# Last attention: dilated groups' scores on 128x32 tiles, queries stored by remainder modulo four, weights added on VectorE

## What is computed

```python
DILATED_GROUPS = ((128, 1), (512, 4), (2048, 16))      # (window, dilation)

def dilated_window_attention(q, k, v, window, dilation):
    """Causal dilated window: query t attends t, t-r, t-2r, ..., t-window.
    Returns normalised output and log-denominator."""
...
def dilated_layer(h, k, v, norm_g, w_in, qnorm_g, w_out, cos, sin):
    proj = rms_norm(h, norm_g) @ w_in
    q, z = jnp.split(proj, [B_QW], axis=-1)
    q = apply_rope(rms_norm(q, qnorm_g), cos, sin)      # 3 groups x 4 heads x 128
    outs, lses = [], []
    for g, (window, dilation) in enumerate(DILATED_GROUPS):
        o_g, l_g = dilated_window_attention(q[:, :, g], k, v, window, dilation)
        outs.append(o_g)
        lses.append(l_g)
    wts = jax.nn.softmax(jnp.stack(lses, axis=0), axis=0)
    o = jnp.einsum('gbsh,gbshd->bshd', wts, jnp.stack(outs, axis=0))
    y = o.reshape(Bsz, S, B_VW) * jax.nn.silu(z.astype(jnp.float32))
    return y.astype(h.dtype) @ w_out
```

## Time and profile before

| | |
|---|---|
| median of 3 runs | 1366.26 us (1366.13 to 1366.35) |
| the profiled execution | 1366.81 us, span in the trace 1365.0 us |
| PE busy | 1354.0 us, 99% of the span |
| DVE, ACT, POOL busy | 854.6, 609.3, 192.3 us |
| granted TensorE clock | 1.00 in each stage shown below |
| queries and attention of the last layer | about 1168 us to 1298 us of the span |

### The profile page before, as it was taken

How to read it: one execution, slowest core, us unless ns; L and a number is a source line. 1 busy time by engine, 2 the same in 40 slices (tenths; PEclk the granted TensorE clock), 3 DMA queues, 4 the chain that set the end, 5 groups by cost and what they waited for, 6 DMA issues and landing times.

```text
span 1365.0 us, 17389 instructions
## 1 busy us (share of the span) xinstructions
PE 1354.0 (99%) x6812; PEld 1108.2 (81%) x6812; DVE 854.6 (63%) x1243; ACT 609.3 (45%) x938; POOL 192.3 (14%) x166
## 2 busy tenths in 40 slices
PE   9999999999999999999999999999999999999998
PEld 7778787888888788888888888788888888787887
DVE  6565666855344797524777356747464666877775
ACT  5264433433245464323444355435554544444551
POOL 0300010222222200000000112011201210244330
PEclk9999999999999999999999999999999999999999
DMA  6322222323352443332333323522224233222132
GB/s 215 113 88 78 78 78 62 93 68 101 95 184 63 139 123 103 114 94 79 105 95 94 119 81 142 155 77 78 63 80 167 82 121 111 78 62 63 47 139 77
DMA packets 37818, 136.57 MB, mean 100 GB/s; under 512 B 4452, under 2 KB 5476, under 8 KB 37096
## 3 DMA queue, kind: packets, MB, share of 16 engines
q1 hardware_dynamic: 37440, 134.39, 31.7%
q10 hardware_dynamic: 296, 1.06, 0.2%
HBM read 129.14 MB, written 6.30 MB: 99 GB/s over the span
## 4 chain that ended last, share of the span: by engine, by line
PE 88%; DVE 8%; issue 1%; ACT 1%; DMA 1%; POOL 0%; DVEq 0%; SPq 0%; ACTq 0%; POOLq 0%
PE ps L205 86%; PE ps L209 3%; DVE WL L152 2%; DVE TT L164 2%; DVE HL L164 1%; DMA kept<-PW 1%; DVE X L152 1%; DVE sm L170 0%; DVE KT L164 0%; DMA raw<-in_wall 0%; ACT HH L202 0%; DVE gS L164 0%; ACT row L202 0%; DVE row L167 0%; ACT VT L202 0%
## 5 line engine op out<-in xcount | busy, mean ns | idle before, releaser
L205 PE MATMUL ps<-HH,WH 128*128 128x512 f32 (+1 forms) x1096 | 437.0, 401 | 1.1 <-DVE HL L164 0.6
L205 PE MATMUL ps<-HL,WH 128*128 128x512 f32 (+1 forms) x1096 | 423.4, 388 | 0.0
L205 PE MATMUL ps<-HH,WL 128*128 128x512 f32 (+1 forms) x1080 | 417.6, 388 | 0.0
L152 DVE TENSOR_TENSOR WL<-raw,WH 128x1024 fp32r<-128x1024 f32 (+1 forms) x221 | 282.1, 1282 | 77.5 <-ACT WH L189 73.4
L189 ACT CAST WH<-raw 128x1024 fp32r<-128x1024 f32 (+1 forms) x222 | 231.3, 1044 | 123.4 <-PE ps L205 101.8
L205 PEld LDWEIGHTS ps<-HH,WH 128*128 128x128 f32 x1096 | 206.4, 188 | 47.7 <-issue 5.1
L205 PEld LDWEIGHTS ps<-HL,WH 128*128 128x128 f32 x1096 | 206.1, 188 | 41.7 <-issue 1.9
L205 PEld LDWEIGHTS ps<-HH,WL 128*128 128x128 f32 x1080 | 202.8, 188 | 42.7
L205 PE MATMUL ps<-PH,WH 128*128 128x512 f32 x424 | 167.1, 394 | 0.0
L205 PE MATMUL ps<-PH,WL 128*128 128x512 f32 x424 | 165.2, 390 | 0.0
L205 PE MATMUL ps<-PL,WH 128*128 128x512 f32 x424 | 165.1, 389 | 0.0
(11 more groups left out here) (227 smaller groups left out, 1476.7 us busy)
## 6 DMA issues: line engine op xcount, KB each, us to landing
raw<-in_wall SPq DMA_DIRECT2D x221, 512.0 KB, 3.6
kept<-PW SPq DMA_DIRECT2D x2, 2048.0 KB, 9.1
PWR<-kept SPq DMA_DIRECT2D x2, 2048.0 KB, 8.3
X<-in_xT SPq DMA_DIRECT2D x8, 256.0 KB, 4.0
X<-in_xT SPq DMA_DIRECT2D x4, 512.0 KB, 5.3
out_T<-X SPq DMA_DIRECT2D x7, 256.0 KB, 2.0
pe<-in_pT SPq DMA_DIRECT2D x2, 512.0 KB, 4.6
MB<-mrow ACTq DMA_DIRECT2D x1, 1024.0 KB, 5.9
```

The costliest lines, as they stand in the source:

```text
L152: return self.put(None if self.e is None else self.e.tensor_tensor(out, x, y, op))
L205: return self.put(None if self.e is None else self.e.matmul(out, l, r, start=start, stop=stop, skip_group_check=True))
```

## The change

Three things are changed together.

1. Queries are stored by class. Within each block of 128 positions, `qt(h, g)` now holds first the 32 positions with remainder 0 modulo 4, then those with 1, 2 and 3 (`by_class`, `by_token`). This is done while writing: VectorE puts the cosine part into the scratch ring `TH` in natural order, and GpSimd's addition writes `QT` in class order. ScalarE's squares go out in class order too, and at the end of a head the factor and the output are brought back to natural order. ScalarE makes a copy `KC` of the keys, sorted by class over all 512 positions, one copy for each head.
2. `scores(i)`: group 0 stays one matmul of 128 queries by `W0` keys. For groups 1 and 2 each class `k` has a matmul of its own: 32 stationary columns (the class's queries), moving the `L/4` keys of that class, into partitions `32k` to `32k+31` of the bank. So eight matmuls take the place of two. All three groups of a step share one bank, and steps alternate between two banks. The score row shrinks from `W0 + 2L` to `W0 + L/2`, and with it the mask, the masking instructions and the exponential.
3. `merge(i)` moves from GpSimd to VectorE. Four additions, one for each class on its 32 partitions, write the sum of groups 1 and 2 to every fourth column of `PB` (zeroed once by GpSimd). A fifth adds the near columns of `PB` to group 0's weights, in place in `SS`. `turn(i)` transposes the near blocks from `SS` and the far ones from `PB`.

```diff
@@ att_sizes, att_groups @@
-            return L, W0, W0 + 2 * L
+            return L, W0, W0 + L // 2
...
-                w, k0 = (W0, L - W0) if g == 0 else (L, 0)
-                so = 0 if g == 0 else W0 + (g - 1) * L
-                mo = (0, 256, 768)[g] + (256 if g == 0 else 512) - w
-                yield g, w, k0, so, mo
+                w = L // 4 if g else W0
+                yield g, w, W0 + (g - 1) * w if g else 0, (256, 384, 512)[g] - w
+        def by_class(x):
+            return x.rearrange("p (n c j) -> p n j c", n=4, c=4)
+        def by_token(x):
+            return x.rearrange("p (n j c) -> p n j c", n=4, c=4)
@@ pe_program, attend: scores @@
-                    for g, w, k0, so, mo in att_groups(n):
-                        s = p.fill(SB[g], ("as", i, g))
-                        p.wait_ge(S.dve, "kt", h)
+                    s = p.fill(SB[i % 2], ("as", i))
+                    p.wait_ge(S.dve, "kt", h)
+                    p.wait_ge(S.act, "kc", h)
+                    for g, w, so, mo in att_groups(n):
                         p.wait_ge(S.pool, "rope", ("q", h, g))
-                        p.matmul(s[:, 0:w], qt(h, g)[:, n * P:(n + 1) * P], KT[:, h, k0:k0 + w],
-                                 True, True).then_inc(("as", i, g))
+                        if g == 0:
+                            p.matmul(s[:, 0:W0], qt(h, 0)[:, n * P:(n + 1) * P], KT[:, h, L - W0:L], True, True)
+                        else:
+                            for k in range(4):
+                                p.matmul(s[32 * k:32 * k + 32, so:so + w], qt(h, g)[:, n * P + 32 * k:n * P + 32 * k + 32],
+                                         KC[:, h, k * P:k * P + w], True, True)
+                    p.then_inc(("as", i))
@@ pe_program, attend: turn @@
-                    p.wait_ge(S.pool, "aw", i)
+                    p.wait_ge(S.dve, "aw", i)
                     for kb in range(n + 1):
-                        p.transpose(s[:, kb * P:(kb + 1) * P], PB[:, kb * P:(kb + 1) * P], ident)
+                        at0 = kb * P - (L - W0)
+                        p.transpose(s[:, kb * P:(kb + 1) * P], near[:, at0:at0 + P] if at0 >= 0 else PB[:, kb * P:(kb + 1) * P], ident)
@@ v_rope_q @@
-            v.scalar_tensor_tensor(u, ps(*name), gn, CS[:, 0, :], MUL, MUL)
+            v.take("TH", ("rope", name))
+            v.scalar_tensor_tensor(th_("rope", name), ps(*name), gn, CS[:, 0, :], MUL, MUL)
@@ dve_program, attend @@
-                            v.wait_ge(S.pool, "aw", i - 2)
-                        v.tensor_tensor_reduce(Sc[:, so:so + w], ps("as", i, g)[:, 0:w], DM[:, mo:mo + w],
+                            v.wait_ge(S.pe, "at", i - 2)
+                        v.tensor_tensor_reduce(Sc[:, so:so + w], ps("as", i)[:, so:so + w], DM[:, mo:mo + w],
...
+                def merge(i):
...
+                    v.wait_ge(S.act, "aexp", i)
+                    if i == 0:
+                        v.wait_ge(S.pool, "no class")
+                    else:
+                        v.wait_ge(S.pe, "at", i - 1)
+                    for k in range(4):
+                        r = slice(32 * k, 32 * k + 32)
+                        v.tensor_tensor(PB[r, k:L:4], Sc[r, W0:W0 + w], Sc[r, W0 + w:tot], ADD)
+                    v.then_inc(("spread", i))
+                    v.wait_ge(S.dve, "spread", i)
+                    v.tensor_tensor(Sc[:, 0:W0], Sc[:, 0:W0], PB[:, L - W0:L], ADD).then_inc(("aw", i))
@@ act_program @@
-            a.activation(sq_("rope", name), ps(*name), ACT.Square)
+            a.activation(by_class(sq_("rope", name)), by_token(ps(*name)), ACT.Square)
...
+            def key_classes(h):
+                a.wait_ge(S.dve, "kt", h)
+                a.copy(KC[:, h, :].rearrange("p (c j) -> p c j", c=4), KT[:, h, :].rearrange("p (j c) -> p c j", c=4)).then_inc(("kc", h))
@@ pool_program @@
-                g.tensor_tensor(PB[:, 0:L], Sc[:, W0:W0 + L], Sc[:, W0 + L:W0 + 2 * L], ADD).then_inc(("aw0", i))
-                g.wait_ge(S.pool, "aw0", i)
-                g.tensor_tensor(PB[:, L - W0:L], Sc[:, 0:W0], PB[:, L - W0:L], ADD).then_inc(("aw", i))
...
+                g.wait_ge(S.act, "aexp", 0)
+                g.memset(PB, 0.0).then_inc("no class")
```

More of the change, by code:

```diff
@@ L1839, in attend @@
                 yield
+                merge(0)
                 for i in range(16):
@@ L1850, in attend @@
                     yield
+                    if i < 15:
+                        merge(i + 1)
                     yield
@@ L3283, in _layout @@
     cmk = np.where(cc >= r, 0, -NEG).astype(f)
-    dms = [np.where(cc >= r, 0, -NEG), np.where(cc <= r, 0, -NEG)]
-    for d in (4, 16):
-        for blk in range(4):
-            dist = (3 - blk) * P + r - cc
-            dms.append(np.where((dist >= 0) & (dist % d == 0), 0, -NEG))
+    row = 4 * (r % 32) + r // 32
+    dms = [np.where(cc >= row, 0, -NEG), np.where(cc <= row, 0, -NEG)]
+    for d in (1, 4):
+        dist = 96 + r % 32 - cc
+        dms.append(np.where((dist >= 0) & (dist % d == 0), 0, -NEG))
     gup = np.zeros((P, 256), f)
```

38 lines of the change are left out of this document (22 added, 16 removed).

## The result

| | before | changed |
|---|---|---|
| median | 1366.26 us (1366.09 to 1366.54) | 1372.86 us (1372.17 to 1373.41) |
| span of the profiled execution | 1365.0 us | 1371.3 us |

The ratio is 1.0051 (95% interval 1.0039 to 1.0063): the changed kernel is slower, by 6.6 us, where a gain of 5.3 us was forecast, and its time lies above the range of 1357.8 to 1366.3 us.

A forecast was written before the change was run, and what follows sets the result against it. TensorE was taken to bound the kernel: -6.9 (scores) + 1.2 (VectorE's order) + 0.45 (key copy) = -5.25 us from the profiled 1366.8 gave 1361.6, stated as 1361.0 us because the median is 0.55 lower; range 1357.8 to 1366.3.

The forecast's parts named there:

- TensorE saves 6.9 us: Score matmuls: cost falls from 23.4 to 16.5 us over four heads, with small tiles overlapping fourfold.
- the forecast switch of 0.35: Scores on TensorE: fixed 0.35 us per step for entering and leaving the small tiles, 5.6 us over sixteen steps.
- the floor of 14.7 ns: Small score matmuls: a record costs at least 14.7 ns, taken for 64 and 32 columns from the linear attention's trace.
- The rival with a common path for weights: Small score matmuls: weight loads share one path, every record costs 27 ns, 6.9 us in all; 1363 us, chance 0.13.
- the one in which the tiles don't overlap: Small score matmuls: column tiles run one after another, scores cost 28.6 us; about 1372 us, chance 0.10.
- The least distance of 25 ns: Small score matmuls: a rule setting about 25 ns between matmuls, 6.5 us instead of 4.9; the forecast sided against it.
- VectorE's sum, 99 us: Score stage: VectorE's work rises from 85.4 to 99 us and fits beside TensorE's 105, counted as no cost.
- Because VectorE still has idle time in each head (1.5 us), I take a value near the low end: VectorE's order: merges delaying the rotation cost 0.3 us a head, 1.2 us, out of 0 to 12.6.
- Squares and rotations with a stride ... I count 0: ScalarE squares and GpSimd rotations, 32-element stride: at worst doubled, 0.6 and 1.3 us per query tile; counted as 0.
- ScalarE's key copy, 0.45 us (0 to 0.6): Before the first query rotation: ScalarE's first key copy delays RT and VectorE's work behind it, adding 0.45 us.
- Third rival, VectorE the bound: Score stage: VectorE needs over 105 us because strided class additions cost more; 1363.5 to about 1370 us, chance 0.15.
- the first rival: Scores on TensorE: the small-tile switch costs half, 2.8 us less, and no stall; 1357.5 to 1358.5 us, chance 0.12.

The follow-up runs named there:

- e10_none: Changed kernel with squares in natural order, key copies on GpSimd and no merge of groups 1 and 2 at all; 1358.2 us.
- e5_pool: Changed kernel with the merge, otherwise as it is, on GpSimd instead of VectorE; 1367.35 us.
- e11_late: Changed kernel with the merge one place later in VectorE's list, behind the next rotation or the next WL; 1370.72 us.
- e1_squares: Changed kernel with ScalarE writing the query squares in natural order, without stride (factors reach the wrong queries); 1367.58 us.
- b2_squares: Kernel before the change, with only the query squares written in class order, 32 elements apart (factors reach wrong queries); 1367.25 us.
- e6_flat: Changed kernel with the merge's class additions on VectorE written without gaps, so weights stand at wrong keys; 1368.3 us.
- e2_keys: Changed kernel with the four class-order key copies made by GpSimd instead of ScalarE; 1372.02 us.
- e3_three: Changed kernel with natural-order squares, key copies on GpSimd and PB zeroed without waiting for the first exponential, merge on VectorE; 1366.49 us.

## Why the prediction was wrong

1. *TensorE saves 6.9 us*: right, and slightly low. Shown by the starts (n = 0, 3: 0.68 and 1.20 us, and 0.99 and 1.10 for n = 1, 2; 7.5 us in all) and by e10_none: 8.2 us between B and C. The records overlap fourfold. Without group 0 the four steps cost 0.46, 0.56, 0.67 and 0.77 us, a straight line: 0.10 us for 32 columns more in sixteen records, on a fixed part of 0.36, which is the forecast switch of 0.35. At 32 columns a record thus adds about 6.5 ns (an estimate from that line), and the floor of 14.7 ns taken from the earlier trace rows does not hold: 0.24 + 0.35 = 0.59 was forecast for n = 0. The rival with a common path for weights is out: by it sixteen records would cost the same with 32 and with 128 columns, and they are 0.31 us apart (0.46 and 0.77). So is the one in which the tiles don't overlap. The least distance of 25 ns in the Trainium skill (TensorE: Matmul & The Clock Gate, "Wait — 56ns, not 53.3ns?") doesn't hold here either: by it they would be about 0.03 us apart.
2. *VectorE's sum, 99 us*: right as a number (99.31), in a stage that grew to 119 us, but by terms that cancel. The merge was sized at 23.1 us and takes 27: the class additions 0.21 to 0.44 us in place of 0.175 to 0.28. Against it, WL fell from 18.5 to 15.8 us, 2.7 where 1.5 was given back, and the short sums `sm<-sm` of 12 columns from 2.8 to 0.7, which had no term.
3. *The step that failed: "Because VectorE still has idle time in each head (1.5 us), I take a value near the low end", 1.2 us of 12.6 for the order.* Idle time in an average says nothing about one place. The loop is rotation (VectorE), square (ScalarE), transposes (TensorE), and the merge stands ahead of its first link, with its own waits for the exponential. Undoing the merge gives 5.5 us (e5_pool), moving it 2.1 (e11_late); all that stands against TensorE's 8.2 us between B and C is 7.6, from merge and squares together. The prediction had named the mechanism, its sign and its upper end, and put its value at the wrong end.
4. *"Squares and rotations with a stride ... I count 0"*: right for the rotations on GpSimd (1.30 us now, 1.29 before), wrong for the squares. It named the worst case, twice the length, and this came (0.60 to 1.09 us). It argued with ScalarE's free time, but the square is a link of the loop: 5.3 us by e1_squares. Alone it would have been nearly right (b2_squares: 0.9 us, and 0.0 between B and C); with the merge ahead of it the slack of the tiles, 0.7 to 3.6 us, was spent. In the profiled execution of e1_squares some 1.5 us of the gain are a stretch of low clock that did not come.
5. *ScalarE's key copy, 0.45 us (0 to 0.6)*: the mechanism was right, the term mis-sized. A copy with that stride takes 1.11 us, and RT moved by 0.85, above the upper end.
6. *No term at all*: the gate behind the last merge (2.6 us) and the two stretches at the low clock (1.5 and 1.4 us). The latter, 2.9 us, are over 40% of the final loss, and each followed a pause of over 2 us that points 3 to 5 made.
7. *Third rival, VectorE the bound*: its outcome came near (1363.5 to 1370; it is 1372.9), its mechanism did not. VectorE idles for 19.7 us. The rival needed 6 us more on the sum, from columns at 2.1 times the price; by e6_flat the 16-byte stride adds 3.9 us, a factor of 1.4 on the columns. (The class additions did take 6 us more than forecast, 20.8 against 14.6, but the sum stayed at 99 by point 2.) The Trainium skill's SBUF — State Buffer, "Door 1: The DMA port swizzle", calls a stride of 4 fp32 the limit of what is free; on VectorE's writes it is not free here (436 ns in place of 346 at 128 columns), but far from a doubling.
8. A slip in the first rival: 1361.0 less 2.8 for the switch and less the stall of 1.2 is 1357.0, not 1357.5 to 1358.5. Nothing rests on it; the fixed part was not cheaper (0.36 us).

Luck has a share in the measured numbers too: the two kernels with a pause of 2.57 us between C and D differ by 1.4 us because the clock fell in one of them.

What stays open: how the 7.6 us between B and C divide between merge and squares, since their waits are shared; and why the clock falls behind one pause and not behind another of the same length.

## What to carry to other kernels

When work leaves the engine that bounds the kernel, ask what slack each link of the loop that feeds it has, from that link's end to the start of what waits for it (here 0.7 to 3.6 us from square to transposes, tile by tile), and lay the added instructions, with their own waits, against that slack, not against an engine's idle share. A strided access on an engine with time to spare is not free if its result is next in such a loop. And count with the price of the clock when a pause grows: of the 22 pauses of 1.9 us and more in this study 15 were followed by a stretch at the lower clock, of 1.4 to 1.5 us each.

## What the runs showed of the hardware

- f32 matmuls with 32 stationary columns in four places overlap fourfold: with 128 moving columns sixteen records and the switch take 1.20 - 0.43 = 0.77 us, with 32 columns 0.46. A column of a quarter adds (0.77 - 0.46)/(16 x 96) = 0.2 ns, a quarter of the 0.826 of one wide record; the fixed part of that line is 0.36 us.
- ScalarE needs 1.09 us instead of 0.60 for 512 columns written 32 elements apart, and 1.11 instead of 0.59 for 512 read 4 elements apart.
- On VectorE an addition from SBUF to every fourth column costs 436 ns where 346 do without gaps (128 columns). Four of 64 columns each, beside a GpSimd addition of 512 columns, take 2.13 us instead of 1.09 (e11_late); the scaling of the keys, 512 columns, takes 1.40 us instead of 0.69 beside GpSimd's copy (e2_keys).
- The granted clock fell to 0.50 behind pauses of 1.90 to 2.63 us of TensorE, at their end or up to 1.3 us after it, and was full again some 3.4 us after it fell. It did so in 15 of 22 such pauses in all profiled executions between 1160 and 1312 us, and the length does not decide it in this range: behind 2.11 us it stayed full in the changed kernel and fell in e2_keys, behind 2.57 us it fell in e1_squares and stayed full in e3_three. Behind the 26 pauses of 1.1 to 1.8 us it never fell.
